# Latent attention with stationary values and an early division, and three moved steps, in a two-block kernel on one Trainium2 core

## The reference

```python
# first block, long convolution (front): all 512 channels, FFT length 2048, done here by split FFTs as matmuls
z = v
for o, gate_o in enumerate((x1, x2)):
    z = gate_o * (bidirectional_long_conv(z, filters[:, o, 0], filters[:, o, 1]) + filt_bias[o] * z)
# second block, state space branch (output_and_states): a scan over the rows, 32 groups of 16 channels
y = Re(C h) + d_skip * u
# second block, latent attention (latent_attention): 4 heads, 192 query/key, 128 value columns, causal
s = einsum('bqhd,bkhd->bhqk', qb, k) * scale          # for each block of 128 queries
s = where(key_pos <= q_pos, s, -inf)
pr = softmax(s, axis=-1)
o = einsum('bhqk,bkhd->bqhd', pr, v)                  # later gated: ym = o * silu(gm)
```

## Time and profile before

| | |
|---|---|
| median of 3 runs | 2110.63 us (2107.69 to 2113.55) |
| the profiled execution's own time | 2110.86 us |
| its span, first to last instruction | 2109.1 us |
| mean granted TensorE clock | 0.990 |
| PE busy | 2031.9 us (96%) |
| DVE busy | 1076.2 us (51%) |
| ACT busy | 642.1 us (30%) |
| latent_attention, first to last matmul | 1739.0 to 1882.2 us |

### The profile page before, as it was taken

One profiled execution on the slowest core, in us unless ns is written; L12 is line 12 of the kernel. 1 busy time (PEld: TensorE's weight loads), 2 busy tenths in 40 slices (PEclk: granted clock), 3 DMA queues, 4 the chain that ended last, 5 costly groups with the idle time before them and its releaser, 6 DMA issues. The chain is left out here.

```text
span 2109.1 us, 23788 instructions
## 1 busy us (share of the span) xinstructions
PE 2031.9 (96%) x9679; PEld 1537.0 (73%) x9679; DVE 1076.2 (51%) x1780; ACT 642.1 (30%) x1054; POOL 258.6 (12%) x134
## 2 busy tenths in 40 slices
PE   5998999999999999999999999999999999999998
PEld 3554557688777777777777888777757776789986
DVE  7789979780022422422422322699975344551365
ACT  4732122122233333333333411111224444350332
POOL 1100012012211111111121212000001200040000
PEclk9999999999999999999999999999999999999999
DMA  9211232213111111111111311522111201021110
GB/s 349 77 60 50 59 101 80 60 31 112 48 31 39 33 41 41 31 51 31 41 31 32 108 55 36 190 90 72 45 33 41 65 11 60 15 116 61 60 41 40
DMA packets 129158, 135.40 MB, mean 64 GB/s; under 512 B 15116, under 2 KB 108375, under 8 KB 128027
## 3 DMA queue, kind: packets, MB, share of 16 engines
q1 hardware_dynamic: 123757, 111.71, 16.8%
q0 software_dynamic: 5152, 22.15, 2.8%
q10 hardware_dynamic: 142, 0.03, 0.0%
HBM read 116.90 MB, written 15.80 MB: 63 GB/s over the span
## 5 line engine op out<-in xcount | busy, mean ns | idle before, releaser
L175 PE MATMUL banks<-h_hi,fr_w_rest 128*128 128x512 f32 x1152 | 465.9, 404 | 9.0 <-DVE h_rest L969 3.8
L176 PE MATMUL banks<-h_rest,fr_w_hi 128*128 128x512 f32 x1152 | 450.9, 391 | 0.0
L177 PE MATMUL banks<-h_hi,fr_w_hi 128*128 128x512 f32 x1152 | 450.3, 391 | 0.0
L175 PEld LDWEIGHTS banks<-h_hi,fr_w_rest 128*128 128x128 f32 x1152 | 217.0, 188 | 80.2 <-issue 32.0
L177 PEld LDWEIGHTS banks<-h_hi,fr_w_hi 128*128 128x128 f32 x1152 | 217.0, 188 | 47.2
L176 PEld LDWEIGHTS banks<-h_rest,fr_w_hi 128*128 128x128 f32 x1152 | 217.4, 189 | 42.7 <-issue 1.2
L1574 DVE COPY arena<-banks 128x768 f32<-128x768 f32 (+1 forms) x64 | 52.8, 825 | 368.5 <-PE banks L1335 368.5
L1255 POOL TENSOR_TENSOR fr_w_rest<-arena,fr_w_hi 128x1024 fp32r<-128x1024 f32 x45 | 107.5, 2390 | 523.5 <-ACT fr_w_hi L1418 523.5
L1441 ACT ACTIVATE arena<-banks,arena 128x512 f32<-128x512 f32 x92 | 63.2, 687 | 260.7 <-PE banks L177 260.6
L823 DVE SCALAR_TENSOR_TENSOR arena<-arena 128x1024 f32<-128x1024 f32 (+4 forms) x120 | 133.6, 1113 | 4.1
L512 PE MATMUL banks<-arena 128*128 128x512 f32 x256 | 115.9, 606 | 8.2 <-issue 4.4
(11 more groups left out here) (374 smaller groups left out, 3421.4 us busy)
## 6 DMA issues: line engine op xcount, KB each, us to landing
arena<-in_w_in SPq DMA_DIRECT2D x80, 512.0 KB, 3.8
arena<-in_w_ada POOLq DMA_DIRECT2D x6, 2048.0 KB, 17.6
arena<-in_w_out SPq DMA_DIRECT2D x10, 512.0 KB, 7.8
arena<-in_x SPq DMA_DIRECT2D x4, 1024.0 KB, 7.1
arena<-in_fwd SPq DMA_DIRECT2D x16, 256.0 KB, 2.7
filter_spectra<-arena POOLq DMA_DIRECT2D x2, 2048.0 KB, 7.5
arena<-in_inv SPq DMA_DIRECT2D x16, 256.0 KB, 2.6
arena<-filter_spectra SPq DMA_DIRECT2D x2, 2048.0 KB, 8.9
```

The source lines that it names most:

```text
L175: nc.tensor.matmul(out, ll, rh, start=start, stop=False)
L176: nc.tensor.matmul(out, lh, rl, start=False, stop=False)
L177: return nc.tensor.matmul(out, lh, rh, start=False, stop=stop)
```

## The change

Three steps are moved, and the attention loop is rewritten.

1. In `front`, TensorE runs the first half of projection 5 before leaves 0 to 3 of the second filter, and its second half between leaves 3 and 4. Before, the first half stood between them and the second half after leaf 7.
2. In `front`, VectorE convolves tile 8 before the product L1061 and no longer after it.
3. In `output_and_states`, the taps go to PSUM banks 6 and 7, and so wait for the last two copies of W (`w_ready` 7 and 8) where they waited for the first two; the states' inputs of banks 0 to 5 no longer wait for the taps' copies, and those of banks 6 and 7 do. VectorE's product with `d_skip` moves behind the first rotation, ahead of the wait for `toeplitz`.
4. In `latent_attention`, ScalarE divides the exponentials themselves, all (i + 1) x 128 columns of them, right behind the exponential pass (`ACT.Copy` with the reciprocal as scale), so VectorE's reciprocal of unit s moves into step s and waits for its exponentials. The transposes come one step later (unit s - 2 in step s), from three buffers in place of two. The values become the stationary operand and the transposed probabilities of four query blocks the moving one: a group of four units is weighted at once, up to 512 columns wide, in 4 or 8 accumulating matmuls, and comes out transposed, so the transposes of the outputs disappear. The two groups of a head are weighted in steps 1 and 2 of the next head; the last group in two pieces.

```diff
@@ -598,12 +598,12 @@
                 if l >= 4:
                     filter_rows(1, l - 4)
             project(4, rows={(0, 2 * n + 1): (1, 4 + n) for n in range(4)})
+            project(5, halves=(0,))
             for l in range(4):
                 forward(3, l, 3, 5, hl_ready, hs_mm, 1)
-            project(5, halves=(0,))
+            project(5, halves=(1,))
             for l in range(4, 8):
                 forward(3, l, 3, 5, hl_ready, hs_mm, 1)
-            project(5, halves=(1,))
             project(6)
             for l in range(8):
                 forward(4, l, 6, 3, zl_ready, zs_mm, 1)
@@ -1057,9 +1057,9 @@
                 multiply(0, l)
             recombine_cyclic(0)
             recombine_negacyclic(0, 7)
+            convolve(8)
             dve.wait_ge(row_ready, 8)
             link(nc.vector.tensor_tensor(tile(6, 0, 8), tile(6, 0, 8), tile(5, 0, 8), ALU.mult), Count(z1_ready))
-            convolve(8)
             split_rows()
             cyclic(z_leaves)
             convolve(9)
@@ -1866,18 +1866,18 @@
                 last.then_inc(w_tr, 1)
             pe.wait_ge(kb_ready, 1)
             for g2 in range(2):
-                pe.wait_ge(w_ready, g2 + 1)
+                pe.wait_ge(w_ready, 7 + g2)
                 half = slice(64 * g2, 64 * g2 + 64)
                 for q in range(4):
                     for ri, taps in enumerate((QR, QN)):
                         for i in range(4):
                             j = 4 * q + i
                             pair = K.at(S5B + 256 * ri + 16 * j, 32)[half, :]
-                            last = nc.tensor.matmul(PS[32 * i:32 * i + 32, g2, q * P:(q + 1) * P], pair, taps[half, j, 0:8, :],
+                            last = nc.tensor.matmul(PS[32 * i:32 * i + 32, 6 + g2, q * P:(q + 1) * P], pair, taps[half, j, 0:8, :],
                                                     start=(ri == 0), stop=(ri == 1))
                 last.then_inc(k_mm, 1)
             for n in range(8):
-                pe.wait_ge(w_ready if n >= 2 else k_ready, n + 1)
+                pe.wait_ge(*(w_ready, n + 1) if n < 6 else (k_ready, n - 5))
                 q, ri = n // 2, n % 2
                 for i in range(4):
                     j = 4 * q + i
@@ -1969 @@ ScalarE
-                nc.scalar.copy(Ksb[:, g2, :, :], PS[:, g2, :].rearrange("p (a b) -> p a b", b=P)).then_inc(k_ready, 1)
+                nc.scalar.copy(Ksb[:, g2, :, :], PS[:, 6 + g2, :].rearrange("p (a b) -> p a b", b=P)).then_inc(k_ready, 1)
@@ -2129,9 +2129,6 @@
                                 K.at(S5TMP, 16, n))
                 n *= 2
-            dve.wait_ge(u_tr, 8)
-            dve.wait_ge(ds_in, 16)
-            link(nc.vector.tensor_tensor(xs, xs, dskip.rearrange("p (g c) -> p g c", c=16).unsqueeze(2).to_broadcast([P, 32, TC, 16]), ALU.mult))
             for q in range(4):
                 js = slice(4 * q, 4 * q + 4)
                 dve.wait_ge(v_mm, 2 * q + 2)
@@ -2147,6 +2144,9 @@
                 tt(tmp[:, 0, :, :], tmp[:, 0, :, :], tmp[:, 1, :, :], ALU.add)
                 tt(tmp[:, 2, :, :], tmp[:, 2, :, :], tmp[:, 3, :, :], ALU.subtract)
                 if q == 0:
+                    dve.wait_ge(u_tr, 8)
+                    dve.wait_ge(ds_in, 16)
+                    link(nc.vector.tensor_tensor(xs, xs, dskip.rearrange("p (g c) -> p g c", c=16).unsqueeze(2).to_broadcast([P, 32, TC, 16]), ALU.mult))
                     dve.wait_ge(toeplitz, 64 * TC)
                 for ri in range(2):
                     for i in range(4):
@@ -2490 @@ latent_attention
-    causal, sb, pt = K.at(YGT, S), K.at(YGT + S, 2, S), K.at(SECW + 4 * S, 2, S)
+    causal, sb = K.at(YGT, S), [K.at(place, S) for place in (GATE, YGT + S, SECW + 4 * S)]
+    past, diagonal = YGT + 2 * S, (ROPE, SECW + 5 * S)
+    assert past + 4 * CH <= YST and GATE + S <= VECS
...
@@ -2503 @@ the list of transposition jobs
+        if 2 <= step < len(units) + 2:
+            i = units[step - 2][1]
+            first_job[step - 2] = len(t_jobs)
+            t_jobs += [("p", step - 2, b0, min(b0 + 4, i + 1)) for b0 in range(0, i + 1, 4)]
         if step < len(units) and units[step][0] + 1 < MLA_HEADS and units[step][1] < UPS:
...
+    def keys(i, b, n=1):
+        if b < i - i % 4:
+            first, step = past + CH * b + P * (i % 4), CH
+        else:
+            first, step = diagonal[i // 4] + 3 * P * (b % 4) + P * (i % 4), 3 * P
+        return K.A[:, first:first + step * n].rearrange("p (b q) -> p b q", b=n)[:, :, 0:P]
+    def group_keys(g, b, n):
+        if b < 4 * g:
+            return 0, K.at(past + CH * b, CH)[:, 0:n * P]
+        return b % 4, K.at(diagonal[g] + 4 * P * (b % 4), (n - b % 4) * P)
+    def group_at(step):
+        h, i = divmod(step - NT, NT)
+        return 2 * h + i - 1 if i in (1, 2) and h >= 0 else None
@@ -2610 @@ TensorE
-                if g >= 2:
-                    pe.wait_ge(t_taken, g - 1)
+                _, u, b0, b1 = t_jobs[g]
+                pe.wait_ge(scaled, u + 1)
+                pe.wait_ge(t_taken, g - 1)
                 for b in range(b0, b1):
-                    src = sb[:, which % 2, b * P:(b + 1) * P] if kind == "p" else orow[:, b, :]
-                    last = nc.tensor.transpose(PS[:, 4 + g % 2, (b - b0) * P:(b - b0 + 1) * P], src, ident)
+                    last = nc.tensor.transpose(PS[:, 4 + g % 2, (b - b0) * P:(b - b0 + 1) * P], sb[u % 3][:, b * P:(b + 1) * P], ident)
                 last.then_inc(t_done, 1)
+            def weighted_values(G, c0, c1):
+                h, g = divmod(G, 2)
+                blocks = 4 * g + c1
+                for b in range(blocks):
+                    c, p = group_keys(g, b, c1)
+                    skip = max(c0 - c, 0)
+                    last = nc.tensor.matmul(PS[:, 6 + G % 2, max(c, c0) * P:c1 * P], vr[:, b, h * P:(h + 1) * P], p[:, skip * P:],
+                                            start=(b == 0), stop=(b == blocks - 1))
+                return last
...
-            for step in range(len(units) + 2):
+            for step in range(len(units) + STAGES):
+                G = group_at(step)
+                final = step == len(units) + STAGES - 1
                 if step < len(units):
                     scores(step)
-                if 1 <= step <= len(units):
-                    u = step - 1
-                    pe.wait_ge(exp_done, u + 1)
+                if G is not None:
+                    pe.wait_ge(t_taken, after_unit(4 * G + 3))
+                    if G >= 2:
+                        pe.wait_ge(y_taken, G - 1)
+                    weighted_values(G, 3 if final else 0, 4).then_inc(pv_done, 1)
+                if step == len(units) + 1:
+                    pe.wait_ge(t_taken, after_unit(len(units) - 2))
+                    pe.wait_ge(y_taken, len(units) // 4 - 2)
+                    weighted_values(len(units) // 4 - 1, 0, 3)
+                if 2 <= step < len(units) + 2:
+                    u = step - 2
                     for g in range(first_job[u], after_unit(u)):
                         transposes(g)
...
                 if next_up(step) is not None:
                     project_up(next_up(step))
@@ -2665 @@ ScalarE, step by step
                     act.wait_ge(nm_ready, step + 1)
-                    nc.scalar.activation(sb[:, step % 2, 0:n], sb[:, step % 2, 0:n], ACT.Exp, bias=nm[:, step:step + 1], scale=QK_SCALE,
+                    nc.scalar.activation(sb[step % 3][:, 0:n], sb[step % 3][:, 0:n], ACT.Exp, bias=nm[:, step:step + 1], scale=QK_SCALE,
                                          accum_out=l[:, step:step + 1]).then_inc(exp_done, 1)
-                if step >= 2:
-                    u = step - 2
-                    h, i = units[u]
-                    act.wait_ge(pv_done, u + 1)
-                    act.wait_ge(rl_ready, u + 1)
-                    if h >= 1:
-                        act.wait_ge(t_done, out_job[h - 1] + 2)
-                    nc.scalar.activation(orow[:, i, :], PS[:, 6 + u % 2, 0:P], ACT.Copy, scale=rl[:, u:u + 1]).then_inc(o_ready, 1)
+                    act.wait_ge(rl_ready, step + 1)
+                    nc.scalar.activation(sb[step % 3][:, 0:n], sb[step % 3][:, 0:n], ACT.Copy, scale=rl[:, step:step + 1]).then_inc(scaled, 1)
                 if next_up(step) is not None:
                     round_up(next_up(step))
                 if step == LAST + 1:
-                    act.wait_ge(t_taken, out_job[1] + 2)
+                    act.wait_ge(y_taken, 4)
                     act.wait_ge(s_done, LAST)
                     act.wait_ge(wout_in, 64)
                 if LAST + 1 <= step < LAST + 5:
@@ -2710 @@ VectorE
...
+            def take_outputs(G):
+                h, cols = G // 2, slice(G % 2 * 512, G % 2 * 512 + 512)
+                dve.wait_ge(pv_done, G + 1)
+                nc.vector.tensor_tensor(ymT[:, h, cols], PS[:, 6 + G % 2, :], gmT[:, h, cols], ALU.mult).then_inc(y_taken, 1)
+            for step in range(len(units) + STAGES):
...
```

(25 more changed lines are left out.)

53 lines of the change are left out of this document (10 added, 43 removed).

## The result

The changed kernel takes 2127.67 us (median of 4 runs, 2125.36 to 2128.16), the kernel before, beside it on the same chip, 2110.97 us (4 runs, 2107.69 to 2113.55). The ratio is 1.008, with a 95% interval of 1.0066 to 1.0093: slower by 16.7 us (14 to 20). The profiled execution of the changed kernel has a span of 2125.6 us, 16.5 more than before's 2109.1. The forecast was 2122.5 us, with a range of 2112 to 2131.

What follows compares the result with a forecast made beforehand. TensorE was taken to set the attention stage and VectorE's chain to lead the front. From 2110.9 us, attention +9.8, projection 5 +3.4, tile 8 0 and taps -1.6 gave 2122.5 us, range 2112 to 2131.

Steps and rivals of the forecast that it cites:

- Price of the division: Attention, ScalarE: a division pass costs as much as an exponential pass, E(i) = 0.40 + 0.107 i us.
- Steps 3 to 7: Middle head in attention: a chain through the division sets the pace, 18.0 us together where they took 19.12.
- Steps 0 to 2: Middle head in attention: they now carry a whole head's weighted sum, 17.7 us where they took 14.92.
- First head: Attention: no weighted sum to make in its steps, so 1.3 us shorter by walking the queues instruction by instruction.
- M + 2E + 1.72: Attention, i < 6: least step time in us from mask pass M and exponential and division passes E; 3.84 to 4.56 for i = 3 to 5.
- Last head: Attention: carries two heads' sums and TensorE waits for divisions and copies; 7.5 us more by walking the queues.
- Rival D: Attention: wide matmuls much cheaper than the row says, 14 us less work; 2110 us, chance 0.03.
- Projection 5: Front stage: idle time at 183.51 filled, but TensorE stalls for `convolve(4)` and the clock halves; +3.4 us, ends 0.7 and 6.0.
- Taps: State stage: taps 1.0 us later, TensorE's 2.48 us idle time gone, outputs earlier; -1.6 us, ends -2.6 and 0.
- A: Whole kernel: TensorE stays the bound and the two steps of lag hide the division; 2099 us, chance 0.10.
- B: Attention chain costs half and no clock stretch falls behind the front stage's stall; 2115 us, chance 0.17.
- C: Clock falls in attention steps 3 to 6 too, and both projection 5 clock stretches are long; 2131 us, chance 0.14.

Runs made afterwards that it cites:

- the experiment on the split: The kernel before with projection 5's first half ahead of leaf 0 and its second half behind leaf 5: 2114.22 us against 2109.07, ratio 1.0023.
- the two experiments: The kernel before with taps and `d_skip` product moved, 2108.28 us; the kernel before with only the `d_skip` product moved, 2106.70 us.
- the first run: The kernel before with the new attention loop alone, the other three places as before: 2120.12 us against 2108.44, ratio 1.0062.

## Why the forecast was right, and where it was off

The sign and its cause are right: the division in the chain is worth about 13 us (10 to 17 by the experiment without it), and nothing else in the change comes near it. The time was 5 us low.

- **Price of the division.** Right within 6 ns at each width. The Trainium skill (ScalarE: Activation LUTs, What ACT_TABLE_LOAD costs) gives 186 ns and 0.833 ns a column, with about 93 ns for a per-partition operand. An estimate from these figures is 386 ns for 128 columns and 1132 for 1024; the trace shows 403 and 1151.
- **Steps 3 to 7.** 18.0 forecast, 18.13 to 18.17 measured, step by step 3.80, 4.15, 4.48, 2.88 and 2.86. The 2.88 was forecast at 2.60: step 6 doesn't wait for the division, but mask 7 waits for its scores, 0.24 us, so TensorE sets that step.
- **Steps 0 to 2.** 17.7 forecast and 17.89 measured at full clock. Each middle head of the changed kernel had 1.7 us more from half clock. I had given that case 0.14 and looked for it in steps 3 to 6, where idle times are spread. There the clock stayed at 1.00 in every trace. It fell in steps 0 to 2, behind the two longest waits of the head:

```profile
1824.87 0.95 PE L2634 MATMUL banks<-arena 128*128 128x128 f32 x7 [0.96 <-DVE arena L2755]
1826.69 2.73 PE L2619 MATMUL banks<-arena 128*128 128x512 f32 x3 [0.87 <-DVE arena L2755]
```

  These are the new waits of step 7 and after that the forecast had at 1.0 and 1.1 us. I priced them and didn't ask what they do to the clock.
- **First head.** -1.3 forecast, -0.1 measured (28.14 against 28.22). The price M + 2E + 1.72 takes the projection at its short form; in steps 0 and 1 it is four records of 512 columns, and step 0 took 3.43 us where the formula gives 2.8. That is half of the miss. Step 1 kept to the formula (3.10 against 3.14), step 6 took 0.28 more as above, and the formula's own sum over the eight steps is only 0.75 us below before's; where the walk found its further 0.5 us the record doesn't show.
- **Last head.** 7.5 forecast, 6.0 measured (39.17 against 33.13). The waits are the ones named, but smaller: 1.31 and 1.88 for 1.6 and 2.1, then 0.94 for 1.1.

```profile
1887.28 0.85 PE L2634 MATMUL banks<-arena 128*128 128x128 f32 x6 [1.31 <-DVE arena L2755]
1890.01 0.95 PE L2634 MATMUL banks<-arena 128*128 128x128 f32 x7 [1.88 <-DVE arena L2755]
...
1898.82 2.05 PE L2643 MATMUL banks<-arena 128*128 128x128 f32 x16 [0.94 <-DVE arena L2755]
```

  The errors of the first and the last head cancel: -0.1 + 2 x 2.0 + 6.0 = 9.9 us at full clock, against 9.8 forecast, and 3.3 us of clock on top.
- **Wide weighted sums.** Rival D, cheap wide matmuls, falls (its 14 us less work would be about 16, with the ratio of 1.6 put on each width). The weight loads between their 512-column records in the changed kernel are 0.43 us apart, the spacing of the earlier trace rows:

```profile
1868.65 0.19 PEld L2643 LDWEIGHTS banks<-arena 128*128 128x128 f32 x1 [0.24 <-issue]
1869.08 0.19 PEld L2643 LDWEIGHTS banks<-arena 128*128 128x128 f32 x1 [0.24 <-issue]
```
- **Projection 5.** 3.4 forecast, 4.9 here and 5.0 alone, inside the ends of 0.7 and 6.0. The stall, its place (205.04) and who ends it are right. What was mis-sized is the clock: it stood at 0.51 for the 7 us around the stall and cost 2.0 us (projection 6 starts 5.0 us late where 3.0 was forecast), then at half again in projection 6 for 1.7; with the 0.7 us that is 4.4, and VectorE's lag at L901 (240.28, now 243.57) grew by 4.5. The forecast's 3.4 had left 2.7 us for the clock, where 3.7 were paid. Leaf 4's own wait, which the experiment on the split laid bare, plays no part here: its inputs were there at 202.15, and without the stall TensorE would have come to it at about 203.3 (an estimate: this half began at 196.58 and took 6.74 us in the kernel before).
- **Tile 8.** 0 forecast, +0.3 here and +0.8 alone, both no more than untouched executions vary by over this stretch. The wait went to 351.39, 4.93 us long, as said.
- **Taps.** -1.6 forecast, -0.7 here, -1.1 alone. The taps came 1.15 us later in both, near the 1.0 forecast. The term that failed is the step from there to the scan: it came 1.4 us later alone and 1.75 here. With the taps left in place it came 0.4 us earlier, so the two experiments put the price of the delay at 1.8 us where I had 1.0.
- **Rivals.** A, TensorE stays the bound, falls by the first run (masks 3 to 8 at 18.1 us). The rule beside it in the Trainium skill (Perfetto Trace Analysis, Identifying the Most-Contended Engine), to go by the engine with the highest occupancy, would have misled: TensorE stood at 95 or 96% in all kernels here, from 2101 to 2135 us. The page has TensorE judged by its weight loads and not by its matmuls; these stood at 71 to 73%, still the highest share in each. B asked for half the chain's price, and that didn't come. C came half true, and its 2131 us is nearer to the measured 2127.67 than my 2122.5: the clock did fall in the attention, in steps 0 to 2 and not in steps 3 to 6 (3.4 us in place of its 6), and part 2 cost 4.9 where it had 6.0.

Of the 4.9 us between the forecast's 11.6 and the 16.5 of the spans, +1.5 is projection 5, +0.9 the taps, +0.3 tile 8, +3.4 attention, which is the clock there, and -1.2 + 2.1 - 2.0 = -1.1 code that nobody touched, for the most part its clock. Together 5.0, 0.1 of it rounding. That much of these last three terms cancels is luck, as it is that the errors of the first and the last head do.

## What to carry to other kernels

When work moves to an idle engine, ask not how busy that engine is but what stands behind the new instruction in its queue and who waits for that: a pass on an engine that is idle for two thirds of the time cost about 13 us. Once the short hand-over (`round_up`, `rest_of_up`, the projection) went ahead of it in all three queues, the kernel with the pass (2105.40 us) was faster than the one without it in the old order (2109.27). What the pass still costs in the new order no run shows. Before a piece of work is pulled forward to fill a wait, look at what it covers where it stands: the two halves of projection 5 covered two later waits, and in both new orders filling 4.4 us brought waits of 5 and 4.5. A saving of work on the busiest engine (4.9 us here by the forecast's rows) doesn't show as long as a chain through the others sets the pace.

## What the hardware showed that I had not expected

- **Where the clock falls isn't fixed by the code.** In steps 0 to 2 of two middle heads with the same instructions and the same waits ahead (0.96 and 0.88 us, 0.95 and 0.87), one ran at 1.00 and one at 0.91 (17.89 and 19.56 us). In the first head of the changed kernel TensorE waited 1.81 us, and the clock stayed at 1.00. In the changed kernel the clock was at half for 3.4 us at 1485.6, in untouched code that ran at 1.00 before. In `second_output` it is the other way round; the first row is of the kernel before, the second of the changed one, both right behind the same kind of wait:

```profile
1884.50:1887.90 3.40, 3.40 (x9) 2.77 (x9) 2.10 (x1) 3.40 (x3) 3.40 (x7) 0.50 0.84 276
```

```profile
1903.00:1908.00 5.00, 5.00 (x22) 5.00 (x21) 3.63 (x2) 5.00 (x4) 4.09 (x8) 1.00 0.91 332
```

  Each such stretch is worth 1.7 to 2.0 us. What decides between the two, with the same idle time before them, stays open.
- **A single trace hides small gains.** The executions differ by up to 2.9 us before the first edit is reached, in part by such stretches in the first 113 us. The effects of 0.5 to 3 us (tile 8, taps, `d_skip`) could be read only between landmarks of the same trace, and the timings confirm no more than their order of size. Untouched code grows or shrinks by as much: up to 0.7 us around tile 8, and 1.7 to 2.0 where a stretch of half clock falls or doesn't.
